# Delta rule: running sums of a head's decays as two float32r products over 512 masked columns, in place of four float32 products

## What is computed

```python
g = -exp(a_log) * softplus(a + dt_bias)            # log decay of a token and head
gc = cumsum(g within a chunk)                      # running sum of the decays
decay[i, j] = exp(gc[i] - gc[j])  for i >= j
a_in = (k k^T) * beta * decay ;  qk = (q k^T) * decay
q_dec = q * exp(gc) ; k_dec = k * exp(gc_last - gc)
# (I + strict_lower(a_in)) is inverted, then the chunks are scanned with a 128x128 state
```

## Time and profile before

| what | value |
| --- | --- |
| median of 3 runs | 2149.07 us (2146.14 to 2149.64) |
| the profiled execution's own time | 2149.31 us |
| its span in the profile | 2147.5 us |
| granted TensorE clock over the span | 0.995 |
| busy: PE, DVE, ACT, POOL | 2098.6, 1213.1, 906.2, 325.7 us |
| the preparation of the delta rule | about 42 to 161 us of the span |

### The profile page before, as it was taken

The page is one execution under the profiler, slowest core; times in us unless marked ns, Lnnn a source line. Parts: engine busy times, 40 slices in busy tenths (PEclk is TensorE's granted clock), DMA queues, the critical chain, the costliest instruction groups (busy, mean ns, idle before and its releaser), DMA issues.

```text
span 2147.5 us, 26841 instructions
## 1 busy us (share of the span) xinstructions
PE 2098.6 (98%) x9776; PEld 1700.2 (79%) x9776; DVE 1213.1 (56%) x1663; ACT 906.2 (42%) x1282; POOL 325.7 (15%) x266
## 2 busy tenths in 40 slices
PE   6999999999999999999999999999999999999999
PEld 5778888878868888887766888888878878888887
DVE  5898755765366666225544566653354465666522
ACT  6883444434244444224564444442242354444411
POOL 0001121220112222001301222220000012222200
PEclk9999999999999999999999999999999999999999
DMA  7323222122212223221211222232222122322321
GB/s 235 94 75 95 82 78 70 49 69 74 97 66 96 92 95 120 95 83 66 69 40 49 88 98 98 98 114 94 86 69 89 60 73 94 98 98 97 115 95 66
DMA packets 81481, 188.96 MB, mean 88 GB/s; under 512 B 19824, under 2 KB 40432, under 8 KB 81392
## 3 DMA queue, kind: packets, MB, share of 16 engines
q1 hardware_dynamic: 81392, 187.75, 26.8%
HBM read 178.28 MB, written 9.44 MB: 87 GB/s over the span
## 4 chain that ended last, share of the span: by engine, by line
PE 92%; DVE 4%; ACT 2%; issue 1%; DMA 0%; POOL 0%; SPq 0%; ACTq 0%; DVEq 0%
PE acc L253 23%; PE acc L255 23%; PE acc L254 23%; PE bank L1726 1%; PE bank L1245 1%; PE bank L229 1%; PE bank L230 1%; PE bank L231 1%; PE acc L2634 1%; PE acc L2633 1%; PE acc L2632 1%; PE bank L2017 1%; PE bank L253 1%; PE bank L254 1%; PE bank L255 1%
## 5 line engine op out<-in xcount | busy, mean ns | idle before, releaser
L253 PE MATMUL acc<-HH,whi 128*128 128x512 f32 x1600 | 643.8, 402 | 6.9 <-DVE wlo L191 4.3
L255 PE MATMUL acc<-HH,wlo 128*128 128x512 f32 x1600 | 625.9, 391 | 0.0
L254 PE MATMUL acc<-HL,whi 128*128 128x512 f32 x1600 | 625.1, 391 | 0.0
L185 ACT ACTIVATE whi<-raw 128x1024 fp32r<-128x1024 f32 (+1 forms) x293 | 324.1, 1107 | 566.9 <-PE acc L255 537.6
L191 DVE TENSOR_TENSOR wlo<-raw,whi 128x1024 fp32r<-128x1024 f32 (+1 forms) x293 | 400.7, 1369 | 283.4 <-ACT whi L185 283.4
L253 PEld LDWEIGHTS acc<-HH,whi 128*128 128x128 f32 x1600 | 302.1, 189 | 73.9 <-DVE wlo L191 9.5
L255 PEld LDWEIGHTS acc<-HH,wlo 128*128 128x128 f32 x1600 | 301.4, 188 | 64.6
L254 PEld LDWEIGHTS acc<-HL,whi 128*128 128x128 f32 x1600 | 302.1, 189 | 62.5 <-issue 4.1
L253 PE MATMUL acc<-FH,whi 128*128 128x512 f32 x528 | 205.8, 390 | 0.0
L254 PE MATMUL acc<-FL,whi 128*128 128x512 f32 x528 | 205.4, 389 | 0.0
L255 PE MATMUL acc<-FH,wlo 128*128 128x512 f32 x528 | 205.4, 389 | 0.0
(11 more groups left out here) (394 smaller groups left out, 2668.0 us busy)
## 6 DMA issues: line engine op xcount, KB each, us to landing
raw<-w SPq DMA_DIRECT2D x257, 512.0 KB, 3.5
raw<-w SPq DMA_DIRECT2D x48, 704.0 KB, 4.0
X<-x SPq DMA_DIRECT2D x4, 512.0 KB, 5.5
x_dram<-small SPq DMA_DIRECT2D x8, 256.0 KB, 4.3
xt_dram<-small SPq DMA_DIRECT2D x8, 256.0 KB, 3.7
a_dram<-l_am SPq DMA_DIRECT2D x8, 256.0 KB, 3.5
l_xt<-xt_dram SPq DMA_DIRECT2D x8, 256.0 KB, 3.3
l_x<-x_dram SPq DMA_DIRECT2D x8, 256.0 KB, 3.2
```

The lines of the kernel that those rows point to most:

```text
L185: nc.scalar.activation(hi[:, 0:kt * P], raw[u % RAW][:, 0:kt * P], ACT.Copy).then_inc(w_hi_ready, 1)
L253: nc.tensor.matmul(a[:, :], wh, tile(hi, k), start=start and k == 0, stop=False)
L254: nc.tensor.matmul(a[:, :], wh, tile(lo, k), start=False, stop=False)
L255: last = nc.tensor.matmul(a[:, :], wl, tile(hi, k), start=False, stop=stop and k == kt - 1)
```

## The change

The decays `t_ld` are split once into a high and a low float32r part by GpSimd (`part_decays`, four instructions, two of them 128x96 and two 128x128). For each head GpSimd makes two tiles of 512 columns (`gate_decays`): the head's decays of the four chunks, each broadcast over 128 columns and multiplied by `upper`, from the high and from the low part. TensorE multiplies a float32r matrix of ones with each, adding up in `bank[2]`: the result is the same running sums on all partitions. GpSimd makes the tiles of head p when the product of head p - 1 has been read (`p_prod` at 3(p-1) + 1). The new tiles lie where no live tile lies: the parts behind the 1024 columns of `whi` and `wlo` that this stage uses, `gb_hi` on an unused tile and `gb_lo` on `l_ors`.

```diff
+        gb_hi, gb_lo = at_tile("l_gb_hi", 4, 1, F32R), place("l_gb_lo", S, tab0 + 664 * 4, F32R)
...
+        ld_hi, ld_lo = whi[0][:, KD * P:KD * P + 96], wlo[0][:, KD * P:KD * P + 96]
+        lower_r, ones_r = whi[1][:, KD * P:(KD + 1) * P], wlo[1][:, KD * P:(KD + 1) * P]
+        t_parted = sem("decay_parts_ready")
+        def part_decays(pool):
+            pool.wait_ge(params_in, ALL_PARAMS)
+            pool.wait_ge(a_dve, 4)
+            nc.gpsimd.tensor_copy(ld_hi, t_ld[:, :]).then_inc(t_parted, 1)
+            pool.wait_ge(t_parted, 1)
+            nc.gpsimd.tensor_tensor(ld_lo, t_ld[:, :], ld_hi.bitcast(F32), ALU.subtract).then_inc(t_parted, 1)
+            nc.gpsimd.tensor_copy(lower_r, lower).then_inc(t_parted, 1)
+            nc.gpsimd.tensor_copy(ones_r, ones).then_inc(t_parted, 1)
         def prep_pool(pool, c):
             nc.gpsimd.memset(l_inv[:, :], 0.0).then_inc(g_zero, 1)
+            part_decays(pool)
+            def gate_decays(p):
+                pool.wait_ge(t_parted, 4)
+                if p:
+                    pool.wait_ge(p_prod, 3 * (p - 1) + GCB)
+                for out, ld in ((gb_hi, ld_hi), (gb_lo, ld_lo)):
+                    nc.gpsimd.tensor_tensor(by_chunk(out), head_of(ld.bitcast(F32), 24, 0, p), each_chunk(upper),
+                                            ALU.mult).then_inc(t_parted, 1)
             pool.wait_ge(g_zero, 1)
+            gate_decays(0)
             pool.wait_ge(z_filled, 32 * NH)
             nc.gpsimd.memset(l_inv[:, 0:1024:33], 1.0).then_inc(g_zero, 1)
+            for p in range(1, NH):
+                gate_decays(p)
...
-                for k in range(NC):
-                    last = nc.tensor.matmul(chunk(bank[2], k), head_col(t_ld, 24 * k, p).to_broadcast([P, P]), upper,
-                                            start=True, stop=True)
-                last.then_inc(p_prod, 1)
+                pe.wait_ge(t_parted, 4 + 2 * p + 2)
+                nc.tensor.matmul(bank[2][:, :], ones_r, gb_hi[:, :], start=True, stop=False)
+                nc.tensor.matmul(bank[2][:, :], ones_r, gb_lo[:, :], start=False, stop=True).then_inc(p_prod, 1)
```

More of the change, by code:

```diff
@@ L1474, in chunk_sums_pe, with at_tile @@
                 nc.tensor.matmul(bank[1][:, 96 * k:96 * k + 96], m, t_ld[:, :], start=True, stop=True).then_inc(a_pe, 1)
-        def at_tile(name, k, n=1):
-            return place(name, n * S, FREE + k * TILE)
+        def at_tile(name, k, n=1, dt=F32):
+            return place(name, n * S, FREE + k * TILE, dt)
         c_tap, c_step, c_silu = sem("l_tap_ready"), sem("l_conv_step"), sem("l_silu_ready")
```

## The result

The kernel with the change took **2154.43 us** (median of 20 runs, 2150.51 to 2156.54). The kernel before took 2152.73 us (median of 20). The ratio is **1.0013**, 95% interval 1.0008 to 1.0019: 2.8 us slower, between 1.7 and 4.1 us (the medians lie 1.7 us apart, the means 2.8). The forecast was 1.3 us slower. Sign and class (within 0.2%) are as forecast; the size is over twice as large. The absolute time is 4 us above the forecast of 2150.4 us mostly because that started from a median of three runs, 2149.07 us, where twenty give 2152.73.

The account below looks back on a forecast made before the run. It took DVE, not TensorE, to bound the stage from head 3's end. Terms 0.75 - 0.88 + 0.57 + 0.75 + 0.05 gave +1.2 us, so 2150.4 us, range 2146.5 to 2155.5.

Parts of the forecast that it names:

- What sets the pace: From head 3's end to the stage's end DVE, not TensorE, sets the time; TensorE's gain counts in heads 0 to 3 at most.
- TensorE's products: At the running sums, two float32r products take 0.46 us in place of 0.90, saving 0.44 us for a head.
- GpSimd blocks DVE, and the taps are free: Beside GpSimd's tiles, a blocked DVE instruction with two SBUF operands loses 0.31 to 0.83 us; taps reading PSUM lose nothing.
- The pair behind head 0: Tiles made behind head 0 hold off l_kn about 0.5 us and l_qn about 0.8; everything behind moves by +0.75 us.
- Behind head 3: Tiles hold off l_qn by 0.3 us and a small inversion instruction by 0.85; slack takes up half: DVE late by +0.57 us.
- Behind head 4: One tile falls on the tap's end or GpSimd's own waiting, one blocks DVE for 0.75 us: +0.75 us.
- Behind heads 5 and 6: DVE is over a microsecond late, so the pairs of tiles fall on the three taps, which do not contend: +0.05 us.
- Rival 1: Heads 3 to 6: every pair of tiles blocks DVE in full, +5.9 to +7.9 us, 2155 to 2157 us; chance 0.14.
- Rival 2: No blocking of DVE; three TensorE savings count before DVE sets the pace from head 3: -1.3 us, 2148.0 us; chance 0.12.
- Rival 3: TensorE sets the pace everywhere in the stage, so all eight savings count: -3.5 us, 2145.8 us; chance 0.04.
- Rival 4: Head 0: TensorE's wait grows from 1.27 to about 2.2 us and the clock falls: +3.0 us in all, 2152.2 us; chance 0.12.
- Rival 5: The new TensorE products run at a float32 price, not as one pass: +4.8 us, 2155 us; chance 0.02.

Follow-up runs that it names:

- on the norms: The changed kernel with each pair of GpSimd tiles held back until l_kn is made: 2155.58 us, 1.0023 to the kernel before, stage +5.14 us.
- the saving alone: The changed kernel with tiles made only for head 0 and read by all heads: 2150.75 us, 0.9999 to the kernel before, stage -1.29 us.
- under the taps: The changed kernel with each pair of tiles held back until DVE is about to run its taps: 2150.26 us, 1.0001, stage -1.29 us.
- made ahead: The changed kernel with own tiles per head, seven made at the start, three more in each of three heads: 2150.62 us, 1.0002, stage -1.40 us.
- late pairs moved: The changed kernel with only the pairs behind heads 3 to 6 held back to fall on DVE's taps: stage 111.79 us, -0.69 us.
- doubled-late kernel: The kernel before with the four float32 products issued twice in heads 4 to 7: 2150.47 us, stage 112.78 us, +0.30 us.

## Why the prediction was right, and where it was wrong

**What sets the pace: right.** "From head 3's end to the end of the stage the clock of the work is DVE": 3.6 us of added TensorE work there cost 0.30, 1.8 us ahead of it cost 1.73.

**TensorE's products: right.** 0.47 us against 0.90, forecast 0.46.

**GpSimd blocks DVE, and the taps are free: right.** A whole tile costs a blocked instruction 0.83 us (48x31 step, 1.03 for 0.20) to 0.86 us (48x207 step, 1.22 for 0.36), forecast up to 0.83; where two tiles block in a row, the second cost 0.74. The taps kept 2.30 us for three. The Trainium skill's rule (SBUF — State Buffer, "Who interferes with whom") calls the shared ports an exclusive lock that, outside its 2-port modes, a DVE instruction meets only with two SBUF inputs; the trace agrees on who contends, and on the lock. The prediction worked out by it that the loser would lose the tile's whole 1.04 us; 0.83 to 0.86 us are added to the record, as it took from the rows. That is no sign against the lock. Take the blocked record's end less the instruction's own length as the start of its own work (an estimate from the rows above): l_kn behind head 4 then starts at 110.33 - 0.69 = 109.64 us, 0.15 us ahead of the end of the tile's record at 109.79; wlo behind heads 5 and 6 0.13 and 0.14 us ahead; the 48x31 step 0.16; the two steps on the norms 0.13 and 0.14. The loser waits to the tile's end each time, and the records of the two overlap by that much. The three such handovers also are the 0.4 us by which the 3.04 us of the earlier trace rows fall short of the four own times, 3.46 us, which the prediction called "about the sum".

**The pair behind head 0: right in mechanism, a little dear.** l_kn became 0.41 us longer and l_qn 0.63, TensorE's wait went from 1.27 to 2.10 us and 0.30 more for l_qn. Net of head 1's saving +0.17 against +0.31.

**Behind head 3: right** (+0.47 against +0.57), on the two instructions named, l_qn and a small inversion step. The remark there that "head 3's own saving is already lost" holds only because this pair blocks: with nothing blocking, it counts (-0.44 at the taps behind it, in the saving alone, under the taps, made ahead and late pairs moved).

**Behind head 4: the size is off.** The prediction let one tile fall on the tap's end or on GpSimd's own waiting and the other block for 0.75 us. Measured +0.99: the first tile held wlo off by its last 0.15, the second waited behind wlo and then cost l_kn the full 0.84.

**The step that failed, in size and by its overlap: "Behind heads 5 and 6: DVE is late by now by over a microsecond against TensorE, and the pairs fall on the three taps ... I take +0.05 us".** Measured +0.59 and +0.35, together 0.94. The pairs do fall on the taps, and DVE was late by 1.19 us, as said. Two things were left out of the working. First, the margin: two tiles need 2.1 us and the taps last 2.30, so the pair is hidden only if it starts in the first 0.2 us of the taps. By the prediction's own numbers it would not: the sums of head 5 started here in the kernel before,

```profile
123.61 1.05 PE L1764 MATMUL bank<-cst,t_ld 128*128 128x128 f32 x8
```

so they would end at 123.61 + 0.46 = 124.07 us, the pair could start at 124.38 (GpSimd follows 0.31 us behind, as 123.01 follows 122.47 + 0.23), and the late taps would start at 122.50 + 1.19 = 123.69. Second, "late against TensorE" doesn't last. From head 4 on TensorE waits for l_kn, and so moves with DVE and carries the pair along. In times of before (1.56 us are added to those of after, for the earlier start of its stage) the sums of head 5 ended at 124.26 us, 0.19 late, and those of head 6 at 140.67 against 139.43, 1.24 late, with the taps late by 1.20 and 1.78. So the pair started 0.87 us behind the taps in head 5 and 0.65 us in head 6, and its second tile stood out at the end both times and held off wlo. The working asked *on what* a pair starts, not *on what it ends*, and took the pair's time as fixed although TensorE's wait had just moved it. With 0.99 and 0.94 in place of 0.75 and 0.05 the prediction's sum of 1.2 us is 2.4 us, against 2.12 in the stage; the early terms and head 3's came out 0.24 us lower than forecast and hid part of the miss. The remaining 0.7 us of the measured 2.8 are of the size of the clock's 0.8, which no term of the prediction held.

**The rivals.** Rival 1 (every pair blocks in full) did not occur, but was the better warning: the pairs behind heads 3 and 4 made DVE's instructions 1.1 and 1.0 us longer, and a wait in another place gives its 1.6. Rival 2's number, -1.3 us, is what is left when the tiles are placed so that none blocks. Rival 3 fell. Rival 4 (the clock falls in head 0) did not occur: the wait grew to 2.10 and 0.30 us, as forecast for it, and the granted clock stayed 1.00 in 45 to 60 us. Its row, the fall at the end of the stage, was also read too closely. Before, the clock fell at about 162.7 us, 1.4 us behind the end of the wait of 2.45 us. After, behind a wait of 2.86 us, it stayed full at first and fell at about 177 us (0.91 and 0.86 in the two windows above). In the doubled-late kernel, where that wait doesn't exist, the first fall came at about 178 us. The Trainium skill (TensorE: Matmul & The Clock Gate, "What's actually happening") ties the clock to how busy the array has recently been; these profiles don't contradict it, but one wait can't be charged with one fall. Its price was a little high too: the 3.4 us at the lower clock there cost some 1.3 us at the 0.39 found above, not 1.8. Rival 5 did not occur.

## What to carry to other kernels

An engine that is 98% busy over the run may be waiting in the very stage that a change touches; doubling its work there, early and late, tells in two short runs whether a saving can count. In these traces work given to GpSimd cost nothing where DVE had slack or ran its taps, which read one operand from PSUM; elsewhere it cost up to 0.86 us a tile. Both ends count: ask when the last tile ends, not only when the first starts, and hold GpSimd back until the PSUM-reading stretch begins rather than let it start at its operand's readiness. If that stretch is there, GpSimd can also take work off DVE under it, and that was worth more here (3.2 us of stage) than the 1.4 us that TensorE's saving brought.

## What was not expected of the hardware

- A whole tile of GpSimd costs the same whatever the size of the blocked instruction: 0.83 us on a 48x31 step of 0.20 us, 0.86 on a 48x207 one of 0.36 us, 0.84 on a 128x512 one of 0.69 us. Small instructions suffer most in proportion.
- GpSimd's record can be twice its own time (2.03 to 2.04 us for 1.05) with nothing shown as a wait; the longer record belongs to the engine that lost.
- The stage repeats to 0.01 us between profiles (114.60 and 114.61; 111.19 both for the saving alone and for the tiles under the taps) while whole runs of one kernel spread over 6 us and more. Most of the spread is the clock: the mean granted clock of a run accounts for 87% of its variance, and a us at the lower clock loses 0.39 us.
